# Attention scores as 64x64 blocks, and the neighbourhood attention's scores moved behind its projection

## The chip, the cores and the metric

The kernel runs on one NeuronCore of a Trainium2 chip. The metric is the device time of one execution in microseconds (us), from launch to end. TensorE (PE) multiplies matrices: it loads a stationary operand and streams a moving one past it, and its products land in PSUM, which has eight banks of 512 float32 columns on 128 partitions. VectorE (DVE), ScalarE (ACT) and GpSimd (POOL) work beside it, each through its own instructions in order. Engines wait for each other by semaphores.

## The reference

Two transformer models run one after the other on a sequence of 512 tokens with 1024 features. The first has two layers of feed-forward, hybrid mixer, feed-forward. Part of the mixer is sliding-window attention:

```python
scores = jnp.einsum('bnqkgd,bnskd->bnkgqs', qb, kb).astype(jnp.float32) * (HEAD_DIM ** -0.5)
```

The second model has two layers. Layer 0 is latent attention (16 heads; a query and a key have 64 plain features and 32 rotary ones, and the rotary key is shared by all heads). Layer 1 is neighbourhood attention (16 heads of 64; each query sees 256 context keys and a window of 256 grid keys). Both have 256 context tokens beside the 512 latent ones:

```python
s = jnp.concatenate([jnp.einsum('bqhd,bkhd->bhqk', qc, k_ctx),
                     jnp.einsum('bqhd,bkhd->bhqk', ql, k_lat)], -1)
p = softmax_f32(s.astype(jnp.float32) * scale).astype(v_lat.dtype)
```

## The kernel before, in words

Weights come by DMA, are split by ACT and POOL into a rounded high part and a low rest, and each projection is three fast matmuls per 128 rows of the contraction (lines 2603, 2604, 2605, called "fills" where they stand between the steps of an attention). The attention's own matmuls are plain float32. Each of those leaves two records of matmul in the trace, one after the other in time for one tile, and where two or four tiles of the array hold different blocks, the records of the tiles start 7 ns or so apart and stream side by side.

The order of TensorE's work in each attention is written out by hand, in one function per attention. A unit is a block of 128 queries of a pair of heads `g = 0, 1`, whose queries and keys lie on rows 0 to 63 and 64 to 127.

Latent attention (`mla_pe`): 4 passes of 12 units, 48 in all: 32 with latent queries, 16 with context queries. For unit u the loop issues `scores(u + 1)`, the first half of the transposition `turn(u, 0)` (line 2106: 64x64 blocks of probabilities against a diagonal that divides by the sum), `weigh(u - 1)` (line 2124: values), one fill into bank 7, and `turn(u, 1)`. Scores of a latent unit are four pairs of matmuls: plain rows with latent keys (L2085) and context keys (L2087), rotary rows with both (L2089, L2091); a context unit has L2080 and L2082. The rotary rows are 32 per head and lie at `h * 32`; the rotary key `kr` stands four times, once per 32 rows. `scores(u)` waits for the exponentials of unit u - 1 (L1426 on ACT).

Neighbourhood attention (`na_pe`): 32 units. Before the loop it issues six fills, `scores(0)` and one fill more. For unit u the loop issues `scores(u + 1)` (L2219, L2222), then the fill number u + 7 into bank 7 (there is one for u = 0 to 25), for which it first waits until the fill before it has been copied out of bank 7, then for u = 27 to 31 parts of the next projection (two to nine matmuls), `turn(u)` (L2236) and `weigh(u - 1)` (L2256). On ACT, `na_act` does for each u, in this order: `exps(u + 1)` (L1513), `fill_out` of fill u + 7 (L1490 to L1500), `copy(u)` (L1521), sometimes the split of a weight panel (L1589). On DVE, `na_dve` does `most(u + 1)` (bias added L3321, maximum L3326), `copy(u)` (L3340), `shares(u + 1)` (L3331, L3332). The lines of PE that the change moves:

```python
for u in range(NA_ALL):
    if u + 1 < NA_ALL:
        scores(u + 1)
    if na_fill(u) is not None:
        pe.wait_ge(sem["fill_out"], b["fill_out"] + u + NA_FIRST + 1)
        fill(u + NA_FIRST + 1, 7)
    ...
    turn(u)
    if u:
        weigh(u - 1)
```

The mixer's attention (`mixer_pe`): 8 units in each of two layers, each with fills, `scores(u + 1)` (L1875, L1877), `turn(u)` (L1894) and `values(u - 1)` (L1909), in this order.

Of the kernel before, what the change touches and what calls it, by code (L numbers as in the profile page):

```python
# [20 lines left out]
ds = bass.ds  # L21

P = 128
# [229 lines left out]
def mla_step(a):  # L253
    wq, wkv = weight_panels(a["mla_w_qb_2"][0]), weight_panels(a["mla_w_kvb_2"][0])
    n = NH // PER
    pairs, units = PER // 2 * 6, PER * 6

    def dma(i, j):

        w, per, first, second = ((wq, DQ, NOPE, ROPE), (wkv, P, NOPE, HD))[j]  # L260
        out = []
        for h in range(PER):
            out.append((("cols", h * first, first), w[:, :, ds(i * (PER * per) + h * per, first)]))
            out.append((("cols", PER * first + h * second, second), w[:, :, ds(i * (PER * per) + h * per + first, second)]))
        return out

    return dict(kind="mla", iters=n, shapes=[(3, PER * DQ), (2, PER * P)], dma=dma,
                totals=dict(fill_made=11 * n, fill_out=11 * n, q_rot=n,
                            s_made=pairs * n, s_max=units * n, s_exp=units * n, s_shared=units * n,
                            turned0=units * n, turned1=units * n, copied0=units * n, copied1=units * n,  # L270
                            s_weighted=pairs * n, s_kept=PER * n, h_hi=KD - 1, h_ready=KD - 1))
# [199 lines left out]
def build(nc, a, out):  # L471
# [101 lines left out]
    mean_m = sb("mean_m", [P, P])  # L573
    eps = sb("eps", [P, 2])
    spare = place[0]
# [64 lines left out]
    kn = sb("kn", [P, 2, T], at=h_at + 11264)  # L640
    kr = sb("kr", [P, T], at=h_at + 17408)
    vals = (sb("vals_even", [P, 6, PER * HD], at=g_raw_at), sb("vals_odd", [P, 6, PER * HD], at=h_at + 26624))
# [679 lines left out]
    def mla_in_act(st, b, act, split_hi):  # L1322
# [39 lines left out]
        for k in (3, 4):  # L1362
            rounded(k)
        act.wait_ge(sem["low_out"], b["low_out"] + 4)

        nc.scalar.activation(kr[:, 0:C], low_pe[:, 0:C], ACT.Copy).then_inc(sem["act_chain"], 1)

# [460 lines left out]
    def mixer_pe(st, b, pe, triple, first_panel):  # L1828
# [31 lines left out]
        def scores(u):  # L1860
            i, nh = u // 2, u % 2
            if u == 0:

                pe.wait_ge(sem["in_evac"], b["in_evac"] + 3)
            else:
                pe.wait_ge(sem["at_s_read"], b["at_s_read"] + u)
            if u == 4:

                pe.wait_ge(sem["in_evac"], b["in_evac"] + 5)
            for m in range(2):  # L1870
                n = 2 * nh + m
                for g in range(2):
                    q = mq[rows_at(g), i, n * P:(n + 1) * P]
                    if n == 0:
                        ins = nc.tensor.matmul(ps_g[:, g, P:2 * P], q, mk[rows_at(g), 0:P], start=True, stop=True)  # L1875
                    else:
                        ins = nc.tensor.matmul(ps_g[:, g, m * 2 * P:(m + 1) * 2 * P], q, mk[rows_at(g), (n - 1) * P:(n + 1) * P], start=True, stop=True)  # L1877
            ins.then_inc(sem["at_s"], 1)
# [126 lines left out]
    def mla_pe(st, b, pe, triple):  # L2005
# [55 lines left out]
        def scores(u):  # L2061
# [12 lines left out]
            qq = slice(q * P, (q + 1) * P)  # L2074
            low_rows = lambda g: slice(g * NOPE, (g + 1) * NOPE)
            rope_rows = lambda g: slice((2 * hp + g) * ROPE, (2 * hp + g + 1) * ROPE)
            first, second = (lambda g: ps_all[:, 2 * g, C:2 * C]), (lambda g: ps_all[:, 2 * g + 1, :])
            if ctx:
                for g in range(2):
                    nc.tensor.matmul(first(g), qcn[low_rows(g), hp, qq], kn[low_rows(g), hp, 0:C], start=True, stop=False)  # L2080
                for g in range(2):
                    ins = nc.tensor.matmul(first(g), qcr[i % 2][rope_rows(g), qq], kr[rope_rows(g), 0:C], start=False, stop=True)  # L2082
            else:
                for g in range(2):
                    nc.tensor.matmul(second(g), qn[low_rows(g), hp, qq], kn[low_rows(g), hp, C:T], start=True, stop=False)  # L2085
                for g in range(2):
                    nc.tensor.matmul(first(g), qn[low_rows(g), hp, qq], kn[low_rows(g), hp, 0:C], start=True, stop=False)  # L2087
                for g in range(2):
                    nc.tensor.matmul(second(g), qt[i % 2][rope_rows(g), qq], kr[rope_rows(g), C:T], start=False, stop=True)  # L2089
                for g in range(2):  # L2090
                    ins = nc.tensor.matmul(first(g), qr[i % 2][rope_rows(g), qq], kr[rope_rows(g), 0:C], start=False, stop=True)  # L2091
            ins.then_inc(sem["s_made"], 1)
# [78 lines left out]
    def na_pe(st, b, pe, triple, sum_squares):  # L2171
# [30 lines left out]
        def scores(u):  # L2202
# [11 lines left out]
            if u >= 2:  # L2214

                pe.wait_ge(sem["s_exp"], b["s_exp"] + u - 1)
            half = lambda g: slice(g * HD, (g + 1) * HD)
            for g in range(2):
                nc.tensor.matmul(ps_all[:, 2 * (u % 2) + g, 0:C], nq[half(g), pair, j * P:(j + 1) * P], nk[half(g), pair, 0:C], start=True, stop=True)  # L2219
            for g in range(2):  # L2220
                kk = nk[half(g), pair, C:T].rearrange("p (r n) -> p r n", n=GRID)[:, :, BAND[j]:BAND[j] + KC_]
                ins = nc.tensor.matmul(ps_all[:, 2 * (u % 2) + g, C:2 * C].rearrange("p (r n) -> p r n", n=KC_), nq[half(g), pair, j * P:(j + 1) * P], kk, start=True, stop=True)  # L2222
            ins.then_inc(sem["s_made"], 1)
# [46 lines left out]
        for u in range(NA_ALL):  # L2270
            if u + 1 < NA_ALL:
                scores(u + 1)
            if na_fill(u) is not None:
# [3 lines left out]
            for c, k in NA_PROJ.get(u, ()):  # L2277
# [950 lines left out]

    def rope(dve, ch, o, x_, swapped):

        V = nc.vector
        ch.step(V.tensor_tensor(o, x_, turns[:, 0, :], ALU.mult))
        ch.link(V.tensor_tensor(turned[:, :], swapped, turns[:, 1, :], ALU.mult))
        return V.tensor_tensor(o, o, turned[:, :], ALU.add)

    def mla_in_dve(st, b, dve, ch):
        V = nc.vector
        for n, (k0, k1, g) in enumerate(((0, 3, col["q_norm"]), (3, 5, col["kv_norm"]))):
# [7 lines left out]
        dve.wait_ge(sem["rope_in"], 48)  # L3246
        dve.wait_ge(sem["pe_rot"], b["pe_rot"] + 1)
        rope(dve, ch, kr[:, C:T], low_pe[:, C:T], ps_s[:, :]).then_inc(sem["pe_key"], 1)

# [6 lines left out]
    def mla_dve(st, b, dve, ch):  # L3256
# [38 lines left out]
        for g in range(2):  # L3295
            shares(0, g)
        U = PASSES * MLA_N
        for u in range(U):
# [58 lines left out]
    def _(dve):  # L3357
# [115 lines left out]

        n_gemv = [0, 0]
        for st in PLAN:
            b = st["base"]
# [241 lines left out]
```

## Time and profile before

| what | value |
|---|---|
| median of 3 runs | 3669.26 us (3668.59 to 3672.66) |
| span of the profiled execution | 3665.2 us |
| its own time as a run | not listed; the median is 4.1 us above the span |
| PE busy | 3609.4 us, 98% of the span |
| DVE, ACT, POOL busy | 1825.1, 1426.8, 1621.2 us |
| granted PE clock | nine tenths or more in each of the 40 slices |

Busy time counts a stretch once, however many records overlap in it. A matmul's record is longer than the time after which the next can start, so what a step costs on PE is read from start to start. A row of the timeline merges instructions of one line: its first column is the start of the first. 64\*128 is a stationary block of 64 rows and 128 columns.

### The profile page before, as it was taken

To read this page: it belongs to the slowest core of one execution; us is meant where nothing else is said; L and a number is where in the kernel's file an instruction comes from. 1 tells how busy PE (TensorE), PEld (TensorE's weight loads), DVE (VectorE), ACT (ScalarE), POOL (GpSimd) and SP (SyncE) were. 2 spreads that over 40 slices of the span, in tenths; PEclk is the share of its full clock that TensorE was granted. 3 is DMA by queue.
4 is the path that set the end of the run, shared out by engine and by line. 5 is a ranking of instruction groups with operands and counts; after the bars stand their busy time and mean duration, and the time that the engine had idled before them with its cause. 6 is when DMAs were issued, how large, how long until landed. Compare 5 with 4: busy or idle time off the path is not lost.

```text
span 3665.2 us, 65989 instructions
## 1 busy us (share of the span) xinstructions
PE 3609.4 (98%) x25844; PEld 3005.3 (82%) x25844; DVE 1825.1 (50%) x3439; ACT 1426.8 (39%) x2027; POOL 1621.2 (44%) x1330
## 2 busy tenths in 40 slices
PE   7999999999999999999999999999999999999998
PEld 6888878888888887888897767888889988888887
DVE  6435565554775655763645444444427433343333
ACT  4322364322432245432234444443436533435333
POOL 2444444445454444445541003345458843334543
PEclk9999999999999999999999999999999999999999
DMA  8665525575555442445420001122245522212332
GB/s 258 190 186 162 149 59 161 184 223 168 183 176 189 151 115 65 157 155 159 139 74 20 15 25 36 58 94 90 90 136 165 159 69 70 75 58 92 92 99 85
DMA packets 560423, 442.81 MB, mean 121 GB/s; under 512 B 60452, under 2 KB 558157, under 8 KB 559949
## 3 DMA queue, kind: packets, MB, share of 16 engines
q1 hardware_dynamic: 560205, 439.73, 39.0%
q8 instruction: 158, 2.59, 0.3%
q14 instruction: 60, 0.49, 0.0%
HBM read 432.65 MB, written 2.83 MB: 119 GB/s over the span
## 4 chain that ended last, share of the span: by engine, by line
PE 92%; DVE 3%; ACT 2%; issue 1%; POOL 1%; SPq 1%; DMA 0%; DVEq 0%; ACTq 0%; POOLq 0%
PE ps_all L2603 26%; PE ps_all L2604 25%; PE ps_all L2605 25%; PE ps_all L2106 2%; PE ps_all L2124 1%; PE ps_all L2588 1%; PE ps_all L2085 1%; PE ps_all L2575 1%; PE ps_all L2089 1%; PE ps_all L2236 1%; PE ps_all L2576 1%; PE ps_all L2256 1%; POOL w_lo L1012 1%; DVE prod_t L3549 0%; PE ps_all L2219 0%
## 5 line engine op out<-in xcount | busy, mean ns | idle before, releaser
L1012 POOL TENSOR_TENSOR w_lo<-raw,w_hi 128x512 fp32r<-128x512 f32 (+2 forms) x1124 | 1341.5, 1225 | 1882.2 <-ACT w_hi L1589 1802.2
L2603 PE MATMUL ps_all<-h_hi,w_hi 128*128 128x512 f32 (+1 forms) x2600 | 1010.4, 389 | 2.8 <-POOL w_lo L1012 2.2
L2605 PE MATMUL ps_all<-h_hi,w_lo 128*128 128x512 f32 (+1 forms) x2600 | 1004.1, 386 | 0.0
L2604 PE MATMUL ps_all<-h_lo,w_hi 128*128 128x512 f32 (+1 forms) x2600 | 1003.9, 386 | 0.0
L1589 ACT ACTIVATE w_hi<-raw 128x2048 fp32r<-128x2048 f32 (+4 forms) x277 | 471.4, 1702 | 1275.5 <-PE ps_all L2605 1268.4
L2603 PEld LDWEIGHTS ps_all<-h_hi,w_hi 128*128 128x128 f32 x2600 | 488.7, 188 | 111.0 <-issue 11.1
L2605 PEld LDWEIGHTS ps_all<-h_hi,w_lo 128*128 128x128 f32 x2600 | 488.6, 188 | 98.7
L2604 PEld LDWEIGHTS ps_all<-h_lo,w_hi 128*128 128x128 f32 x2600 | 488.9, 188 | 96.9
L2603 PE MATMUL ps_all<-hid_hi,w_hi 128*128 128x512 f32 (+1 forms) x1282 | 473.2, 369 | 2.1 <-POOL w_lo L1001 1.7
L2605 PE MATMUL ps_all<-hid_hi,w_lo 128*128 128x512 f32 (+1 forms) x1282 | 469.5, 366 | 0.0
L2604 PE MATMUL ps_all<-hid_lo,w_hi 128*128 128x512 f32 (+1 forms) x1282 | 469.4, 366 | 0.0
L3375 DVE SCALAR_TENSOR_TENSOR ps_all<-g_raw,c_col,ps_all 128x256 f32<-128x256 f32 x832 | 335.7, 482 | 0.0
L2603 PEld LDWEIGHTS ps_all<-hid_hi,w_hi 128*128 128x128 f32 x1282 | 241.7, 188 | 43.0 <-POOL w_lo L1001 2.2
L2604 PEld LDWEIGHTS ps_all<-hid_lo,w_hi 128*128 128x128 f32 x1282 | 241.7, 189 | 39.8 <-issue 0.5
L2605 PEld LDWEIGHTS ps_all<-hid_hi,w_lo 128*128 128x128 f32 x1282 | 241.7, 189 | 39.2
L3577 DVE SCALAR_TENSOR_TENSOR x<-ps_all,modc,x 128x512 f32<-128x512 f32 (+1 forms) x91 | 68.0, 747 | 413.3 <-PE ps_all L2605 407.4
L3549 DVE TENSOR_TENSOR prod_t<-gate_t,ps_all 128x1024 f32<-128x1024 f32 x44 | 53.7, 1220 | 265.5 <-PE ps_all L2605 265.5
L3552 DVE TENSOR_TENSOR hid_lo<-prod_t,hid_hi 128x1024 f32 (+3 forms) x71 | 100.6, 1417 | 107.1 <-ACT hid_hi L1705 107.1
L2603 PE MATMUL ps_all<-c_hi,w_hi 128*128 128x256 f32 x400 | 114.7, 287 | 2.5 <-DVE prod_t L3549 2.5
L3193 DVE SCALAR_TENSOR_TENSOR prod_t<-ps_all,colv,prod_t 128x511 f32<-128x511 f32 (+1 forms) x54 | 33.1, 655 | 163.1 <-ACT prod_t L1756 163.1
L2604 PE MATMUL ps_all<-c_lo,w_hi 128*128 128x256 f32 x400 | 113.8, 284 | 0.0
L2605 PE MATMUL ps_all<-c_hi,w_lo 128*128 128x256 f32 x400 | 113.5, 284 | 0.0
(460 smaller groups left out, 5129.0 us busy)
## 6 DMA issues: line engine op xcount, KB each, us to landing
raw<-in_w_ffn_gu_dram SPq DMA_DIRECT2D x88, 1024.0 KB, 5.2
g_raw<-in_w_mod_dram SPq DMA_DIRECT2D x66, 1024.0 KB, 7.4
raw<-in_ffn_w_in_dram SPq DMA_DIRECT2D x54, 1024.0 KB, 5.0
g_raw<-in_ada_w_dram SPq DMA_DIRECT2D x48, 1024.0 KB, 5.3
raw<-in_w_ffn_down_dram SPq DMA_DIRECT2D x32, 768.0 KB, 4.7
raw<-in_w_ffn_down_dram SPq DMA_DIRECT2D x32, 640.0 KB, 4.3
raw<-in_ffn_w_out_dram SPq DMA_DIRECT2D x22, 768.0 KB, 4.7
raw<-in_ffn_w_out_dram SPq DMA_DIRECT2D x20, 640.0 KB, 4.3
```

The costliest lines, as they stand in the source:

```text
L1012: ins = nc.gpsimd.tensor_tensor(v(w_lo), raw_view(st, i, j)[:, first:end, :], v(w_hi).bitcast(F32), ALU.subtract)
L1589: nc.scalar.activation(w_view(w_hi, j % 2, st["shapes"][j]), raw_view(st, i, j), ACT.Copy).then_inc(sem["w_split_hi"], 1)
L2085: nc.tensor.matmul(second(g), qn[low_rows(g), hp, qq], kn[low_rows(g), hp, C:T], start=True, stop=False)
L2089: nc.tensor.matmul(second(g), qt[i % 2][rope_rows(g), qq], kr[rope_rows(g), C:T], start=False, stop=True)
L2106: ins = nc.tensor.matmul(ps_all[keys_, 4 + qh, t * HD:(t + 1) * HD], prob[n % 2][rows_, g, w], diag[rows_, n % 2, g, rows_], start=True, s ...
L2603: nc.tensor.matmul(o, whi, mhi, start=first, stop=False)
L2604: nc.tensor.matmul(o, whi, mlo, start=False, stop=False)
L2605: return nc.tensor.matmul(o, wlo, mhi, start=False, stop=last)
L3375: ins = nc.vector.scalar_tensor_tensor(o, w, s, sofar, ALU.mult, ALU.add)
L3549: nc.vector.tensor_tensor(prod_t[:, :, 0:N], gate_t[:, :, 0:N], other, ALU.mult).then_inc(sem["product"], 1)
L3552: nc.vector.tensor_tensor(hid_lo[:, w].rearrange("p (c n) -> p c n", c=2), prod_t[:, :, 0:N], hid_hi[:, w].rearrange("p (c n) -> p c n", c ...
L3577: nc.vector.scalar_tensor_tensor(v, ps_d[:, j, 0:N], modc[:, ds(st["gate"] + j + i * 2, 1)], v, ALU.mult, ALU.add).then_inc(sem[f"down{j}" ...
```

## The change

Scores in all three attentions are made in quarters: the 128 queries are cut in two halves, each half goes to its own 64 columns of the array and 64 partitions of PSUM, and the block is 64x64. So that the rotary rows fill 64 too, the rotary query columns are placed so that heads 0 and 2 lie on rows 0 to 63 and heads 1 and 3 on rows 64 to 127, and the rotary key is kept in two copies, each with the rows of the head that is not meant set to zero by a mask of ones and zeros (two new columns of `eps`, eight memsets at the start). DVE makes the first copy before the units (`rope_keys`) and the second after the shares of unit 0 (`rope_keys_odd`); ACT's copy of the context part goes. In the neighbourhood attention `scores(u + 1)` is issued after the fill and the projection parts, right ahead of `turn(u)`; nothing changes there on ACT or DVE.

```diff
+            place = h if j else h // 2 + 2 * (h % 2)
+            out.append((("cols", PER * first + place * second, second), w[:, :, ds(i * (PER * per) + h * per + first, second)]))
...
-        act.wait_ge(sem["low_out"], b["low_out"] + 4)
-        nc.scalar.activation(kr[:, 0:C], low_pe[:, 0:C], ACT.Copy).then_inc(sem["act_chain"], 1)
...
+                    for qh in range(2):
+                        q = mq[rows_at(g), i, n * P + qh * HD:n * P + (qh + 1) * HD]
+                        if n == 0:
+                            ins = nc.tensor.matmul(ps_g[rows_at(qh), g, P:2 * P], q, mk[rows_at(g), 0:P], start=True, stop=True)
+                        else:
+                            ins = nc.tensor.matmul(ps_g[rows_at(qh), g, m * 2 * P:(m + 1) * 2 * P], q, mk[rows_at(g), (n - 1) * P:(n + 1) * P], start=True, stop=True)
...
+            if u == MLA_N // 2:
+                pe.wait_ge(sem["pe_key"], b["pe_key"] + 1)
...
+            first, second = (lambda g, h: ps_all[low_rows(h), 2 * g, C:2 * C]), (lambda g, h: ps_all[low_rows(h), 2 * g + 1, :])
+            def quarters(o, q_, k_, start):
+                for g in range(2):
+                    for h in range(2):
+                        ins = nc.tensor.matmul(o(g, h), q_[low_rows(g), q * P + h * NOPE:q * P + (h + 1) * NOPE], k_[low_rows(g), :], start=start, stop=not start)
+                return ins
...
+                quarters(first, qcn[:, hp, :], kn[:, hp, 0:C], True)
+                ins = quarters(first, qcr[i % 2], kr_ctx[hp], False)
...
+                quarters(second, qn[:, hp, :], kn[:, hp, C:T], True)
+                quarters(first, qn[:, hp, :], kn[:, hp, 0:C], True)
+                quarters(second, qt[i % 2], kr_lat[hp], False)
+                ins = quarters(first, qr[i % 2], kr_ctx[hp], False)
...
+                for qh in range(2):
+                    nc.tensor.matmul(ps_all[half(qh), 2 * (u % 2) + g, 0:C], nq[half(g), pair, queries(qh)], nk[half(g), pair, 0:C], start=True, stop=True)
...
         for u in range(NA_ALL):
-            if u + 1 < NA_ALL:
-                scores(u + 1)
...
                 proj_part(st["following"], pe, triple, c, k)
+            if u + 1 < NA_ALL:
+                scores(u + 1)
             turn(u)
...
+    def rope_keys(dve, ch, b):
         V = nc.vector
-        ch.step(V.tensor_tensor(o, x_, turns[:, 0, :], ALU.mult))
-        ch.link(V.tensor_tensor(turned[:, :], swapped, turns[:, 1, :], ALU.mult))
-        return V.tensor_tensor(o, o, turned[:, :], ALU.add)
+        mask = [eps[:, 2 + m:3 + m] for m in range(2)]
+        dve.wait_ge(sem["rope_in"], 48)
+        dve.wait_ge(sem["low_out"], b["low_out"] + 4)
+        ch.step(V.scalar_tensor_tensor(kr_lat[0][:, :], low_pe[:, C:T], mask[0], turns[:, 0, :], ALU.mult, ALU.mult))
+        V.tensor_scalar(kr_ctx[0][:, :], low_pe[:, 0:C], mask[0], None, ALU.mult)
+        dve.wait_ge(sem["pe_rot"], b["pe_rot"] + 1)
+        ch.link(V.tensor_tensor(turned[:, :], ps_s[:, :], turns[:, 1, :], ALU.mult))
+        V.scalar_tensor_tensor(kr_lat[0][:, :], turned[:, :], mask[0], kr_lat[0][:, :], ALU.mult, ALU.add).then_inc(sem["pe_key"], 1)
+    def rope_keys_odd(dve, ch):
+        V = nc.vector
+        mask = eps[:, 3:4]
+        ch.link(V.scalar_tensor_tensor(kr_lat[1][:, :], low_pe[:, C:T], mask, turns[:, 0, :], ALU.mult, ALU.mult))
+        V.tensor_scalar(kr_ctx[1][:, :], low_pe[:, 0:C], mask, None, ALU.mult)
+        V.scalar_tensor_tensor(kr_lat[1][:, :], turned[:, :], mask, kr_lat[1][:, :], ALU.mult, ALU.add).then_inc(sem["pe_key"], 1)
...
+        rope_keys_odd(dve, ch)
...
+        for m in range(2):
+            for q in range(PER):
+                ch.step(nc.vector.memset(eps[q * Q32:(q + 1) * Q32, 2 + m:3 + m], 1.0 - abs(q % 2 - m)))
```

## Rows read from the trace of the kernel before

**Rows 1.** The page: chain that ended last, by engine

```profile
PE 92%; DVE 3%; ACT 2%; issue 1%; POOL 1%; SPq 1%; DMA 0%; DVEq 0%; ACTq 0%; POOLq 0%
```

**Rows 2.** Latent scores: records, ns min/median/max; idle of PE before L2085, times

```profile
L2085 PE MATMUL ps_all<-kn,qn x128: 589/626/694, 1937.5 to 2240.7; 64*128 64x512 f32 x128
...
  ACT prob_even L1426: 3.7, 5
  ACT prob_odd L1426: 1.8, 6
```

**Rows 3.** Timeline of PE, one latent unit: start, us, work, records

```profile
2000.39 0.93 PE L2106 MATMUL ps_all<-diag,prob_odd 64*64 64x64 f32 x48
2001.25 1.13 PE L2085 MATMUL ps_all<-kn,qn 64*128 64x512 f32 x4
2002.21 0.60 PE L2087 MATMUL ps_all<-kn,qn 64*128 64x256 f32 x4
2002.74 1.13 PE L2089 MATMUL ps_all<-kr,qt_even 32*128 32x512 f32 x4
2003.70 0.60 PE L2091 MATMUL ps_all<-kr,qr_even 32*128 32x256 f32 x4
2004.23 0.93 PE L2106 MATMUL ps_all<-diag,prob_even 64*64 64x64 f32 x48
```

**Rows 4.** Timeline of PE, a context unit's transposition

```profile
1975.78 0.46 PE L2106 MATMUL ps_all<-diag,prob_even 64*64 64x64 f32 x16
```

**Rows 5.** Float32 matmuls of the whole array, back to back (line 2404)

```profile
L2404 PE MATMUL ps_all<-squares,mean_m x16: 378/379/379, 2495.2 to 2498.4; 128*128 128x256 f32 x16
...
L2404 PE MATMUL ps_all<-squares_h,mean_m x16: 590/593/593, 2729.2 to 2735.7; 128*128 128x512 f32 x16
```

**Rows 6.** Timeline of PE, scores and transposition in the mixer

```profile
1376.73 1.13 PE L1877 MATMUL ps_all<-mk,mq 64*128 64x256 f32 x8
```

**Rows 7.** Timeline of DVE at the start of the latent units

```profile
1948.05 0.96 DVE L3277 TENSOR_REDUCE stat<-ps_all 128x1 f32<-128x768 f32 x1 [4.10 <-PE ps_all L2091]
```

**Rows 8.** Timeline of PE, one round of the neighbourhood attention

```profile
3038.93 0.70 PE L2219 MATMUL ps_all<-nk,nq 64*128 64x256 f32 x4
...
3040.00 0.50 PE L2603 MATMUL ps_all<-h_hi,w_hi 128*128 128x512 f32 x1
...
3045.68 1.16 PE L2236 MATMUL ps_all<-diag_n,prob_n 64*64 64x64 f32 x64
3046.77 0.66 PE L2256 MATMUL ps_all<-prob_nt,nv_even 128*64 128x128 f32 x8
...
3047.80 0.70 PE L2219 MATMUL ps_all<-nk,nq 64*128 64x256 f32 x4
```

**Rows 9.** Timeline of DVE, then of ACT, in the same round

```profile
3040.11 0.70 DVE L3321 TENSOR_TENSOR ps_all<-ps_all,bias_m 128x512 f32<-128x512 f32 x1 [0.40 <-PE ps_all L2222]
...
3042.18 0.69 ACT L1513 ACTIVATE prob_n<-ps_all,stat 128x512 f32<-128x512 f32 x1 [3.55 <-DVE stat L3326]
...
3043.43 0.20 ACT L1513 ACTIVATION_READ_ACCUMULATOR prob_n<-ps_all,stat 128x1 f32 x1
3045.79 0.60 ACT L1498 ACTIVATE nk<-ps_all 128x512 f32<-128x512 f32 x1 [2.17 <-PE ps_all L2605]
```

**Rows 10.** Waits of PE in the neighbourhood attention's stretch (2930 to 3250)

```profile
PE ps_all L2236 <- DVE diag_n L3332: 0.2, 1, 0.2
```

**Rows 11.** Timeline, a late round without a whole fill

```profile
3206.44 0.20 ACT L1513 ACTIVATION_READ_ACCUMULATOR prob_n<-ps_all,stat 128x1 f32 x1
3206.54 0.60 ACT L1521 ACTIVATE prob_nt<-ps_all 128x512 f32<-128x512 f32 x1
...
3207.22 0.69 DVE L3321 TENSOR_TENSOR ps_all<-ps_all,bias_m 128x512 f32<-128x512 f32 x1
...
3211.30 0.69 DVE L3321 TENSOR_TENSOR ps_all<-ps_all,bias_m 128x512 f32<-128x512 f32 x1
3211.43 0.46 PE L2236 MATMUL ps_all<-diag_n,prob_n 64*64 64x64 f32 x16
```

**Rows 12.** Timeline of PE, two idle gaps between projections

```profile
550.83 0.51 PE L2603 MATMUL ps_all<-yl_hi,w_hi 128*128 128x512 f32 x1 [1.94 <-POOL w_lo L1012]
...
1457.92 0.74 PE L2603 MATMUL ps_all<-yl_hi,w_hi 128*128 128x512 f32 x1 [1.96 <-POOL w_lo L1012]
```

**Rows 13.** Windows behind those gaps: busy us of PE, PEld, DVE, ACT, POOL; PEclk; DMA

```profile
1458.00:1461.40 3.40, 3.40 (x8) 2.67 (x9) 0.00 (x0) 1.01 (x2) 3.36 (x3) 0.50 0.64 210
...
550.10:553.50 3.40, 2.67 (x12) 2.23 (x13) 0.24 (x1) 1.84 (x3) 3.21 (x4) 1.00 0.42 125
```

More of the change, by code:

```diff
@@ L263, in dma @@
             out.append((("cols", h * first, first), w[:, :, ds(i * (PER * per) + h * per, first)]))
-            out.append((("cols", PER * first + h * second, second), w[:, :, ds(i * (PER * per) + h * per + first, second)]))
+            place = h if j else h // 2 + 2 * (h % 2)
+            out.append((("cols", PER * first + place * second, second), w[:, :, ds(i * (PER * per) + h * per + first, second)]))
         return out
     return dict(kind="mla", iters=n, shapes=[(3, PER * DQ), (2, PER * P)], dma=dma,
-                totals=dict(fill_made=11 * n, fill_out=11 * n, q_rot=n,
+                totals=dict(fill_made=11 * n, fill_out=11 * n, q_rot=n, pe_key=1,
                             s_made=pairs * n, s_max=units * n, s_exp=units * n, s_shared=units * n,
@@ L573, in build @@
     mean_m = sb("mean_m", [P, P])
-    eps = sb("eps", [P, 2])
+    eps = sb("eps", [P, 4])
     spare = place[0]
@@ L640, in build @@
     kn = sb("kn", [P, 2, T], at=h_at + 11264)
-    kr = sb("kr", [P, T], at=h_at + 17408)
+    kr_lat = (sb("kr_lat_even", [P, S], at=h_at + 17408), sb("kr_lat_odd", [P, S], at=hid + 47104))
+    kr_ctx = (sb("kr_ctx_even", [P, C], at=h_at + 19456), sb("kr_ctx_odd", [P, C], at=tmp + 15360))
     vals = (sb("vals_even", [P, 6, PER * HD], at=g_raw_at), sb("vals_odd", [P, 6, PER * HD], at=h_at + 26624))
@@ L1872, in scores @@
                 for g in range(2):
[L1873 to L1877, printed above, removed]
+                    for qh in range(2):
[4 more added lines that the diff above has]
+                            ins = nc.tensor.matmul(ps_g[rows_at(qh), g, m * 2 * P:(m + 1) * 2 * P], q, mk[rows_at(g), (n - 1) * P:(n + 1) * P], start=True, stop=True)
             ins.then_inc(sem["at_s"], 1)
@@ L2078, in scores @@
+            def quarters(o, q_, k_, start):
[3 more added lines that the diff above has]
+                return ins
             if ctx:
[L2079 to L2082, printed above, removed]
-            else:
[L2084 to L2091, printed above, removed]
@@ L2217, in scores @@
             half = lambda g: slice(g * HD, (g + 1) * HD)
+            queries = lambda qh: slice(j * P + qh * HD, j * P + (qh + 1) * HD)
             for g in range(2):
-                nc.tensor.matmul(ps_all[:, 2 * (u % 2) + g, 0:C], nq[half(g), pair, j * P:(j + 1) * P], nk[half(g), pair, 0:C], start=True, stop=True)
+                for qh in range(2):
+                    nc.tensor.matmul(ps_all[half(qh), 2 * (u % 2) + g, 0:C], nq[half(g), pair, queries(qh)], nk[half(g), pair, 0:C], start=True, stop=True)
             for g in range(2):
                 kk = nk[half(g), pair, C:T].rearrange("p (r n) -> p r n", n=GRID)[:, :, BAND[j]:BAND[j] + KC_]
-                ins = nc.tensor.matmul(ps_all[:, 2 * (u % 2) + g, C:2 * C].rearrange("p (r n) -> p r n", n=KC_), nq[half(g), pair, j * P:(j + 1) * P], kk, start=True, stop=True)
+                for qh in range(2):
+                    ins = nc.tensor.matmul(ps_all[half(qh), 2 * (u % 2) + g, C:2 * C].rearrange("p (r n) -> p r n", n=KC_), nq[half(g), pair, queries(qh)], kk, start=True, stop=True)
             ins.then_inc(sem["s_made"], 1)
@@ L3245, in mla_in_dve @@
                 ins.then_inc(sem["low_full"], 1)
-        dve.wait_ge(sem["rope_in"], 48)
-        dve.wait_ge(sem["pe_rot"], b["pe_rot"] + 1)
-        rope(dve, ch, kr[:, C:T], low_pe[:, C:T], ps_s[:, :]).then_inc(sem["pe_key"], 1)
+        rope_keys(dve, ch, b)
     def share(dve, ch, s_, ready, o):
```

4 lines of the change are left out of this document (removed).

## The prediction

> **What bounds the kernel now.** I read the chain of waits first: TensorE holds 92% of it [rows 1], so its time sets the end, and a change is worth what it adds to or takes from TensorE's sequence, start to start. Then I read the two attentions' stretches for TensorE's own waits. In the latent attention it waits for the exponentials 11 times, 5.5 us in all [rows 2]; in the neighbourhood attention its one wait inside the loop is 0.2 us [rows 10]. Both are bound by TensorE, with little room to spare in the first. Last I read single rounds on the timelines, for what lies between two kinds of matmul, and for the time at which ACT and DVE do what TensorE will ask for next.
>
> **Latent scores as quarters.** A float32 record of the whole array costs 0.43 us for 512 columns (6.5 us over 15 steps) and 0.215 for 256 [rows 5]. The two heads already stream side by side: four records of 512 columns take 0.96 us, not 1.7 [rows 3]. Four quarters side by side stream the same columns in the same time, so the blocks themselves gain nothing; what goes is the price of changing the block shape. A latent unit's scores take 2004.23 - 2001.25 = 2.98 us [rows 3] and stream 4 x 0.43 + 4 x 0.215 = 2.58: 0.40 over. The transposition's 48 records take 0.86 us to the next start [rows 3]; 16 take 0.46 where 48 take 0.93 [rows 4], so 32 cost 0.47, 48 cost 0.70, and 0.16 is the price of coming and going. With one shape from `turn(u, 1)` through both scores to the next `turn` all of it goes once a unit: 0.56 us, for 48 units 26.9. (L2085 has 128 records, four a unit: 32 latent units [rows 2]; the other 16 are context units, with the same three changes of shape.)
>
> At the 11 places where TensorE already waits for exponentials, what is saved ahead of the scores only lengthens the wait: the 0.16 and the 0.10 by which the last step (2003.70 to 2004.23, 0.53) exceeds its 0.43 [rows 3]. 11 x 0.26 = 2.9 comes off: **-24.0 us**. Bounds: if quarters of 512 columns streamed only two at a time, 2.58 would become 5.16 and everything would be slower by far (a rival below); no row shows four blocks with a moving operand this long. The nearest row is the transposition, where groups of four records cost 0.47/8 = 0.059 us for a double pass over 64 columns, which is the full rate (0.43/8 = 0.054). I take full rate.
>
> The Trainium skill's page "TensorEngine Tiling (Array Packing)", Key Properties, says that changing the tiling mode drains the engine. By a drain alone, about 0.10 us a change as in that last step, the sum would be 3 x 0.10 x 48 = 14.4 us; the trace shows nearly twice that, because the second load behind a change isn't hidden either, and I go by the rows.
>
> **Mixer.** The same for `scores` and `turn` alone: 1377.80 - 1376.73 = 1.07 us [rows 6] against 4 x 0.215 = 0.86 gives 0.21. Two layers of 8 units: **-3.2 us** (0 to -4).
>
> **Keys on DVE.** The first copy adds one short operation ahead of `pe_rot` and drops ACT's; the queries' rotation and the evacuation of the keys stand behind it, so nothing or a few tenths. The second copy's three operations lie behind the shares of unit 0, where DVE idles 4.10 us before the next maximum [rows 7]; three such operations, at 0.7 us each like a bias addition of 512 columns [rows 9], are 2.1. TensorE asks for them only at unit 6. Without that cover they would cost 2.1 once. Memsets and the order of query columns: before and beside the first loads, nothing. Sum 0 (-0.5 to +2).
>
> **Neighbourhood scores moved behind the fill.** This is the term that decides. As quarters they save one change of shape a round, 0.2 us. But look at ACT's order: `exps(u + 1)`, then the copying out of fill u + 7. In the round shown the scores come first (3038.93), the exponentials are over at 3043.63 while the fill still runs (3040.00 to 3045.68), and the fill is copied out at 3045.79, at once [rows 8, 9]. `turn`, `weigh` and the next scores hide the copy, and the next fill finds bank 7 free. After the change the scores come behind the fill. The fill is complete, but ACT stands in `exps` and waits for these scores' maximum; the next fill waits for ACT. From scores to next fill the chain is now: to the bias addition 1.18 [rows 8, 9], less 0.05 for the entry in one shape; to the first exponential 2.07; both exponentials to the next ACT operation 1.35 (the read at 3043.43 plus 0.10, as in the late round [rows 9, 11], less 3042.18); the copy 0.60 [rows 9]; hand-over about 0.05, my estimate. Together 5.20 us. TensorE's own work there is scores 0.91, `turn` 1.04, `weigh` 1.03 [rows 8]: 2.98. It waits 2.2 us.
>
> A round was 3047.80 - 3038.93 = 8.87 us [rows 8]. It becomes 5.68 (the fill, start to start) + 5.20 = 10.88: +2.01. There are 26 fills in the loop, and each but the first waits: 25 x 2.01 = 50.3. Round 0 has no `weigh` to lie beside the chain (+1.0), and the first fill loses the scores ahead of it (-0.3). Behind the last fill nothing long covers unit 26: from its scores to its `turn` the chain needs 1.13 + (3211.43 - 3207.22) = 5.34 us [rows 11] where TensorE has 0.91 + 1.04 + 1.03 + 0.91 = 3.9; with the round behind it I take +1.9. The last rounds go in DVE's and ACT's own circle, 3211.30 - 3207.22 = 4.08 us [rows 11], and gain nothing. Sum **+52.9 us** (45 to 58: the chain may be shorter or longer by 0.2 a round).
>
> **The clock.** A 1.96 us gap of TensorE was followed by a stretch at a granted clock of 0.50, that is 1.2 GHz instead of 2.4; a gap of 1.94 was not [rows 12, 13]. The gaps to come are of this size, 2.2 us. The low stretch was 3.4 us, and would fall on a fill, so it costs 3.4 x 0.5 = 1.7 us each. From 0 (none of 25) to 42.5 (all). One in two of the gaps shown led to it; since each one lengthens its round and shifts the next against whatever the clock goes by, I take 10: **+17 us**.
>
> On this the Trainium skill speaks the other way: "TensorE: Matmul & The Clock Gate", in its closing table of goals, asks only that idle gaps stay below a length which these gaps do not reach. By it this term would be 0; the row of the 1.96 us gap disagrees.
>
> **Sum.** -24.0 - 3.2 + 0 + 52.9 + 17.0 = +42.7 us. On the profiled execution's span that is 3665.2 + 42.7 = 3707.9; the median of the runs is 4.1 above that span, so I forecast 3712 us.
>
> **Rivals.**
> (A) The same wait, but the clock stays up: 3669.3 + 25.7 = 3695. For it: the 1.94 us gap. Against: the 1.96 us one. 27%.
> (B) The same, and the clock falls after nearly every gap: 3669.3 + 25.7 + 42.5 = 3737. Against it: each stretch of low clock moves the next gap. 9%.
> (C) The other side: the wait doesn't come, because ACT's copy is ready in time. It decides at a chain of 2.98 us from scores to next fill; below that only savings are left: 24 + 3.2 + 31 rounds x 0.2 = 33 us faster, 3636. For it: TensorE waits for almost nothing there now, and the exponentials end 2 us ahead of the fill. Against it: that lead is measured from scores which start before a 5.68 us fill; ACT works in order, and its maximum alone takes 3.2 us from the start of the scores (1.13 + 2.07). 6%.
> (D) Quarters with long moving operands stream two at a time. Then 32 x 2.58 + 16 x 0.86 + 32 x 0.86 + 16 x 0.86 = 138 us more: about 3850. Against it: the transposition's rate. 4%.
>
> **How the numbers follow.** My forecast has 50%, the rivals 46%; the remaining 4% are mixtures, half of them near no change. Anything beyond 0.2% (7 us) a measurement of this kernel can tell from no change. Faster: C, 0.06. Same: 0.02. Slower: all else, 0.92. The range reaches down to A with its NA term at the lower end (3695 - 8, and 3 for the latent term: 3684) and up to B with 5 to spare (3742). It leaves out C and D and the fringes of A and B, together under 2 in 10.
>
> **What would show it.** In the profile after: fills of line 2603 in the neighbourhood attention sit idle before their first record, released by ACT's copies, about 25 times and 2.2 us each; rounds of 10.9 us, or 12.6 with a low clock; granted clock below 1 between about 2930 and 3290. Latent scores with starts 2.58 us apart from the next transposition, and no extra step at the rotary rows. The prediction is wrong if those fills start without idle time (C), if a quarter's group of four takes 0.86 us (D), or if the latent attention shrinks by less than 20 us because DVE or ACT takes the bound there.

## The result and the profile after

The changed kernel takes 3722.1 us, the median of 4 runs (3720.6 to 3723.4), where the kernel before takes 3668.9 on the same chip (3667.5 to 3672.7): a ratio of 1.0147, 95% interval 1.0133 to 1.0162. It is slower by 53 us; the forecast was 3712, the range 3684 to 3742. The profiled execution's span is 3721.0 us against 3665.2.

I divide the span's difference of 55.8 us by stretches of TensorE, each from the start of the first scores to the start of the last record of a transposition:

| stretch | before | after | difference | forecast |
|---|---|---|---|---|
| latent attention | 323.6 | 304.6 | -19.0 | -24.0 |
| mixer, two layers | 77.4 + 77.3 | 2 x 76.8 | -1.2 | -3.2 |
| neighbourhood attention | 260.8 | 333.4 | +72.6 | +69.9 (52.9 order, 17 clock) |
| all the rest | | | +3.4 | 0 |

The page of the kernel after, the chain that ended last: TensorE held 92% of it before [rows 1].

```profile
PE 88%; DVE 5%; ACT 3%; issue 2%; POOL 1%; SPq 1%; DMA 0%; DVEq 0%; ACTq 0%; POOLq 0%
```

The chain now runs over DVE and ACT at more places. The waits of TensorE in the neighbourhood attention say where (2944 to 3278; line waited for, releaser: us in total, times, longest). I show the entries that ACT's copies of a fill end; the others come to 4.0 us in 5 waits, nearly all in the last rounds. Before, the list held one entry inside the loop, of 0.2 us [rows 10]:

```profile
PE ps_all L2608 <- ACT nk L1497: 16.1, 7, 3.1
PE ps_all L2608 <- ACT nq L1494: 13.7, 7, 2.2
PE ps_all L2608 <- ACT nv_odd L1489: 8.6, 4, 2.2
PE ps_all L2608 <- ACT nk L1499: 6.7, 3, 2.2
PE ps_all L2608 <- ACT nv_odd L1501: 4.4, 2, 2.2
PE ps_all L2608 <- ACT nv_even L1489: 4.3, 2, 2.2
PE ps_all L2608 <- ACT nv_even L1501: 2.2, 1, 2.2
```

Those are 56.0 us in 26 waits. Every one is the first matmul of a fill that waits for ACT's copying out of the fill before it. One round on TensorE's timeline (start, us, work, records, idle time before):

```profile
3018.02 0.66 PE L2223 MATMUL ps_all<-nk,nq 64*64 64x256 f32 x8
3018.50 0.61 PE L2227 MATMUL ps_all<-nk,nq 64*64 64x256 f32 x8
3018.93 1.11 PE L2241 MATMUL ps_all<-diag_n,prob_n 64*64 64x64 f32 x64
3019.98 0.66 PE L2261 MATMUL ps_all<-prob_nt,nv_even 128*64 128x128 f32 x8
3020.46 0.61 PE L2261 MATMUL ps_all<-prob_nt,nvb_even 128*64 128x128 f32 x8
3023.23 0.50 PE L2608 MATMUL ps_all<-h_hi,w_hi 128*128 128x512 f32 x1 [2.16 <-ACT nq L1494]
```

And ACT's in the same round, from the first exponential to the copy that TensorE waits for:

```profile
3021.24 0.69 ACT L1512 ACTIVATE prob_n<-ps_all,stat 128x512 f32<-128x512 f32 x1 [6.18 <-DVE stat L3343]
3021.83 0.19 ACT L1512 ACTIVATION_READ_ACCUMULATOR prob_n<-ps_all,stat 128x1 f32 x1
3021.92 0.68 ACT L1512 ACTIVATE prob_n<-ps_all,stat 128x512 f32<-128x512 f32 x1
3022.49 0.20 ACT L1512 ACTIVATION_READ_ACCUMULATOR prob_n<-ps_all,stat 128x1 f32 x1
3022.58 0.60 ACT L1494 ACTIVATE nq<-ps_all 128x512 f32<-128x512 f32 x1
```

The copy of `nq` takes 0.60 us, and its data were complete at about 3018.1, when the fill ended. It starts 4.5 us later because ACT stood ahead of it, idle for 6.18 us, waiting for the maximum of scores that had only just been made. Before, the same kind of copy started 0.1 us after the fill's end [rows 8, 9].

### The profile page after: what moved, and what is told of

It reads as the page before. It is cut to its first block, busy times and chain, and to the rows that moved or that the text cites. A ratio compares the mean times of both kernels' runs of the same rounds, so it can differ in the third digit from the quotient of the medians.

```text
span 3721.0 us, 68048 instructions
## 1 busy us (share of the span) xinstructions
PE 3602.6 (97%) x26868; PEld 3010.8 (81%) x26868; DVE 1820.4 (49%) x3451; ACT 1418.1 (38%) x2026; POOL 1620.1 (44%) x1330
## 4 chain that ended last, share of the span: by engine, by line
PE 88%; DVE 5%; ACT 3%; issue 2%; POOL 1%; SPq 1%; DMA 0%; DVEq 0%; ACTq 0%; POOLq 0%
PE ps_all L2608 26%; PE ps_all L2609 25%; PE ps_all L2610 25%; PE ps_all L2083 3%; PE ps_all L2108 1%; PE ps_all L2126 1%; PE ps_all L2593 1%; DVE stat L3343 1%; PE ps_all L2580 1%; PE ps_all L2581 1%; ACT prob_n L1512 1%; POOL w_lo L1014 1%; DVE ps_all L3338 1%; DVE prod_t L3569 0%; PE ps_all L2223 0%
## 5 line engine op out<-in xcount | busy, mean ns | idle before, releaser
L1512 ACT ACTIVATE prob_n<-ps_all,stat 128x512 f32<-128x512 f32 x64 | 43.4, 683 | 226.4 <-DVE stat L3343 226.3
L3338 DVE TENSOR_TENSOR ps_all<-ps_all,bias_m 128x512 f32<-128x512 f32 x32 | 22.4, 698 | 208.0 <-PE ps_all L2227 208.0
```

The source lines that it names most:

```text
L1512: ins = nc.scalar.activation(prob_n[:, u % 2, g, :], ps_all[:, 2 * (u % 2) + g, :], ACT.Exp, bias=at(1), accum_out=at(2))
L3338: V.tensor_tensor(pair[:, :, C:2 * C], pair[:, :, C:2 * C], bias_m[:, n % BIAS_AHEAD, :, :], ALU.add).then_inc(sem["s_biased"], 1)
```

## The experiments

**1. The two halves of the change apart.** The first kernel is the changed one with the scores back ahead of the fill; the second is the kernel before with only the move.

```
e1 (the kernel after)                     e2 (the kernel before)
  for u in range(NA_ALL):                   for u in range(NA_ALL):
+     if u + 1 < NA_ALL:                  -     if u + 1 < NA_ALL:
+         scores(u + 1)                   -         scores(u + 1)
      ... fill, projections ...                 ... fill, projections ...
-     if u + 1 < NA_ALL:                  +     if u + 1 < NA_ALL:
-         scores(u + 1)                   +         scores(u + 1)
      turn(u)                                   turn(u)
```

> The changed kernel with one part undone: the neighbourhood attention's scores(u + 1) stand again ahead of the fill; all quarters and the two masked keys stay. Theory (the loss is the order, the quarters gain): latent units about 18 us shorter than before, mixer 1 to 2, neighbourhood 32 x 0.05 = 1.6 for the shorter entry into 64x64 blocks; 3669 - 21 = 3648 us (3643 to 3655), no fill of the neighbourhood attention idle for ACT's copies. Rival (the quarters themselves cost there, or the masked keys do): at or above 3669, with neighbourhood rounds longer than 8.87 us.

> The kernel before with one part of the change: scores(u + 1) of the neighbourhood attention behind the fill, everything else as before (64x128 blocks). Theory: as many changes of block shape a round as before, so the whole wait and nothing saved there: 25 rounds x 2.06 + 4 = 55 us, and 8 to 14 stretches of low clock at 1.7 us: 3669 + 75 = 3744 us (3725 to 3760). Rival (the order does no harm by itself): 3669 within 0.2%.

Measured: quarters in the old order 3649.5 us, 0.9949 (0.9936 to 0.9963) of before; the order alone 3744.6, 1.0210 (1.0194 to 1.0225). Apart they come to -19.3 and +75.8, together +56.5, against +53.2 for both at once, which is within the intervals. The neighbourhood attention takes 259.6 us in the first and 333.8 in the second, which has 11 stretches of 3.4 us at the lower clock, as the kernel after has. So the quarters help, the move hurts, and neither needs the other. The move alone shows the same waits, a little shorter, since the old block shape keeps TensorE busy 0.1 to 0.2 us longer in a round. The first of these lines is the order alone's; before it stands the last record of `weigh`:

```profile
3026.24 0.61 PE L2256 MATMUL ps_all<-prob_nt,nvb_even 128*64 128x128 f32 x8
3028.88 0.50 PE L2603 MATMUL ps_all<-h_hi,w_hi 128*128 128x512 f32 x1 [2.04 <-ACT nk L1500]
```

**2. The wait taken away on ACT's side, the move kept.** If the cause is ACT's order, and not the place of the scores as such, then swapping two calls on ACT removes the wait.

```
  for u in range(NA_ALL):            # na_act
+     fill_out(u + NA_FIRST + 1, 7)
      if u + 1 < NA_ALL:
          exps(u + 1)
-     fill_out(u + NA_FIRST + 1, 7)
      copy(u)
```

> The changed kernel with two lines of ACT exchanged in the neighbourhood attention: fill_out of fill u + 7 ahead of exps(u + 1). Theory (the fill waits only because ACT stands in exps ahead of the copy): the idle time before the fills goes, rounds of 8.87 - 0.2 = 8.67 us, no low clock there: about 3722 - 72 - 6 = 3644 us (3638 to 3652), faster than before and than the kernel with the old order. Rival (the wait comes from the late scores by another way, the maximum on DVE or the bank): at least 20 us of idle time before fills stay, 3690 or more.

Measured: 3648.3 us, 0.9946 (0.9932 to 0.9959); the neighbourhood attention 259.2 us, 74.2 less than in the kernel after. TensorE's timeline, then ACT's:

```profile
3008.55 0.66 PE L2223 MATMUL ps_all<-nk,nq 64*64 64x256 f32 x8
3009.04 0.61 PE L2227 MATMUL ps_all<-nk,nq 64*64 64x256 f32 x8
3009.47 1.11 PE L2241 MATMUL ps_all<-diag_n,prob_n 64*64 64x64 f32 x64
3010.51 0.66 PE L2261 MATMUL ps_all<-prob_nt,nv_even 128*64 128x128 f32 x8
3011.00 0.61 PE L2261 MATMUL ps_all<-prob_nt,nvb_even 128*64 128x128 f32 x8
3011.53 0.50 PE L2608 MATMUL ps_all<-h_hi,w_hi 128*128 128x512 f32 x1
```

```profile
3008.66 0.60 ACT L1497 ACTIVATE nk<-ps_all 128x512 f32<-128x512 f32 x1 [3.61 <-PE ps_all L2610]
3011.78 0.69 ACT L1512 ACTIVATE prob_n<-ps_all,stat 128x512 f32<-128x512 f32 x1 [2.52 <-DVE stat L3343]
```

The order of TensorE's work is that of the kernel after; the copy now starts at 3008.66, right behind the fill's last record (3008.24 to 3008.63), and the next fill starts without idle time. ACT's place in line was the whole of the 25 waits in the rounds; the 0.7 us of the first fill stay. The kernel's total is 4 us above what I had put down, and the list of TensorE's waits of this kernel in 3150 to 3250 says where a part of it lies:

```profile
PE ps_all L2241 <- DVE diag_n L3349: 1.9, 3, 1.3
PE ps_all L2608 <- POOL h_lo L1021: 1.4, 1, 1.4
```

These lie in the last rounds, where no whole fill covers the way from scores to `turn`. In the rounds that have a fill the kernel gains 0.2 us each against the kernel before, as put down (8.66 for 8.87, and 8.93 for 9.12).

**3. The late rounds given their old order.** From the kernel above, in rounds without a fill (from 26 on) the scores go ahead again; in a second kernel, from round 25 on, and ACT's calls with them.

```
e5: if na_fill(u) is None and u + 1 < NA_ALL: scores(u + 1)   # ahead of the fill
    ...
    if na_fill(u) is not None: scores(u + 1)                  # ahead of turn(u)
e9: the same with u >= 25 and u < 25; ACT: exps(u + 1) first where u >= 25
```

> The kernel with the copy first, and in the rounds without a whole fill (u = 26 to 31) the scores again ahead of the parts of the next projection. The fast order for the fill rounds saved 0.2 us each of 25 there, yet the whole stretch was no shorter than with the old order (259.2 us against 259.6), so some 4 us must go in the last rounds. Theory (there DVE's and ACT's circle is the bound, and late scores lengthen it): 255.5 us for the stretch, 3648.3 - 4 = 3644.5 us. Rival (the last rounds are no longer for another reason, ACT's high parts or POOL's): 3648, the stretch 259.

> The kernel with the copy first, with scores ahead of the fill and the copy behind the exponentials from u = 25 on instead of u = 26. Theory (behind the last fill, the transposition of unit 26 waits 1.3 us for DVE's diagonal because nothing long lies between its scores and itself; with the scores ahead of that 3 us fill the wait goes): neighbourhood stretch 257.9 - 1.2 = 256.7 us, the whole 3644 us, the fastest of all. Rival (the wait moves to the next transpositions, since DVE and ACT have their own circle of 4.08 us there): 257.9, 3645.4.

Measured: 3645.4 us (0.9937, 0.9923 to 0.9950) and 3646.4 us (0.9942, 0.9928 to 0.9955). The neighbourhood attention takes 257.9 and 256.9 us. The transposition of round 26 still waits for its diagonal matrix in the first, half as long in the second. TensorE's timelines of the two, a line from each:

```profile
3180.03 1.16 PE L2241 MATMUL ps_all<-diag_n,prob_n 64*64 64x64 f32 x64 [1.31 <-DVE diag_n L3351]
```

```profile
3182.55 1.16 PE L2244 MATMUL ps_all<-diag_n,prob_n 64*64 64x64 f32 x64 [0.64 <-DVE diag_n L3354]
```

The late rounds hold a part of the loss: 1.3 us come back, where I had put down 3.7, then another 1.0, where I had put down 1.2. In e9 the wait is halved and not gone. The totals of the two can't be told apart. With e9, e5 is the fastest kernel of the study, 23 us below the kernel before and 77 below the one after; from e1 it differs by 4 us, of which 1.7 are its shorter neighbourhood attention and 1.8 a latent attention without one low clock (below).

**4. The gap filled with other work.** The clock's share is told from the wait's by keeping the wait and giving TensorE something to do in it. Ahead of the fill two matmuls (in a second kernel one) of 512 columns write to a bank that nobody reads at that time.

```
  if na_fill(u) is not None:
+     if u:
+         pe.wait_ge(sem["s_exp"], b["s_exp"] + u)
+         for r in range(2):         # e7: one matmul
+             nc.tensor.matmul(ps_all[:, 2 * ((u + 1) % 2), :], mean_m, h_hi[:, 0:S], ...)
      pe.wait_ge(sem["fill_out"], b["fill_out"] + u + NA_FIRST + 1)
```

> The changed kernel with two float32 matmuls of 512 columns (0.43 us a record, four records, 1.7 us) put on TensorE ahead of each wait for ACT's copy, into a bank of scores that is free; they compute nothing that is used. Theory (low clock follows the idle gap): gaps of about 0.5 us are left, the wait ends when it did, rounds of 10.9 us; the low stretches within the neighbourhood attention go, at most 2 left, 3722 - 20 = 3702 us (3697 to 3708). Rival (the clock falls because the small blocks of the attention load the array little, whatever the gap): the low stretches stay, 3722.

> The changed kernel with one float32 matmul of 512 columns (0.86 us) ahead of each wait for ACT's copy, where the kernel with filled gaps had two; it computes nothing that is used. Gaps of about 1.35 us are left. Theory (low clock follows gaps of the size of 1.9 us and more): no low stretch in the neighbourhood attention or hardly one, 3706 us as with two. Rival (each gap has its chance, in proportion to its length): 6 to 8 low stretches, 3715 to 3718.

Measured: 3706.3 us with two (1.0104, 1.0088 to 1.0119), 3707.1 with one (1.0105, 1.0089 to 1.0120); the neighbourhood attention 316.5 and 318.1 us. TensorE's timeline with two, the end of a gap:

```profile
3017.26 1.98 PE L2280 MATMUL ps_all<-h_hi,mean_m 128*128 128x512 f32 x4
3019.49 0.50 PE L2611 MATMUL ps_all<-h_hi,w_hi 128*128 128x512 f32 x1 [0.25 <-ACT nq L1494]
```

From scores (3014.28) to fill the way is 5.21 us, as in the kernel after (3018.02 to 3023.23): the added matmuls change nothing of the wait's end. Only the granted clock differs. The windows over the whole stretch (us, then busy us of PE, PEld, DVE, ACT and POOL, granted clock, DMA share, GB/s), of the kernel after, of the one with two matmuls, of the one with one:

```profile
2944.00:3278.00 334.00, 274.09 (x4006) 231.57 (x4007) 101.03 (x160) 103.23 (x219) 106.64 (x112) 0.94 0.21 57
```

```profile
2945.00:3262.00 317.00, 304.85 (x4107) 233.47 (x4107) 101.13 (x161) 103.43 (x220) 106.53 (x112) 1.00 0.22 60
```

```profile
2943.00:3262.00 319.00, 285.37 (x4059) 225.86 (x4059) 101.05 (x160) 103.34 (x219) 106.99 (x112) 0.99 0.22 59
```

In the kernel after, 11 stretches of 3.4 us at the lower of the two levels, 1.2 GHz, follow upon 25 gaps, 24 of about 2.2 us and the first of 3.1. With both matmuls the gaps are mostly 0.25 us and no stretch follows. With one they are mostly 1.1 us and one stretch is left, at 2962.7, behind the longest gap, that of the first round:

```profile
2962.45 0.39 PE L2610 MATMUL ps_all<-ch_hi,w_hi 128*128 128x256 f32 x1 [2.06 <-ACT nk L1497]
```

The first gap is one of the eleven, so 10 of the 24 gaps of 2.2 us led to a low stretch; in e2, with gaps of 2.0 us and a first one of 2.9, it is 11 of 25 again. The waits end at the same place in all three kernels here, so it is TensorE's idleness in them that brings the clock down, and the 16.9 us between the kernel after and the one with two matmuls are the clock's (333.4 - 316.5): 1.54 us for each of the 11. The length of the gap alone doesn't decide: the gap of 1.94 us that had no low stretch behind it before [rows 12, 13] is 1.94 to 1.96 us long in all eleven kernels, and has one in e2, e4, e5 and e8. One such stretch of the kernel after, behind its gap and the window ahead of it:

```profile
2997.20:3000.60 3.40, 1.24 (x14) 1.00 (x11) 1.60 (x4) 2.42 (x6) 0.57 (x1) 1.00 0.01 2
3000.70:3004.10 3.40, 3.40 (x19) 3.40 (x18) 0.00 (x0) 0.00 (x0) 0.00 (x0) 0.51 0.02 5
```

The first window is the gap, 1.24 us busy of 3.40; in the second TensorE is busy throughout at a granted clock of 0.51, in 19 records.

**5. The rotary rows as before.** From e1, the widened rows go back to 32x128 blocks (with the single keys' buffer, ACT's copy and the old order of the query columns), so that each latent unit again has two changes of block shape around them. The edit for a latent unit's rows:

```
- quarters(second, qt[i % 2], kr_lat[hp], False)
- ins = quarters(first, qr[i % 2], kr_ctx[hp], False)
+ for g in range(2):
+     nc.tensor.matmul(ps_all[:, 2 * g + 1, :], qt[i % 2][rope_rows(g), qq], kr[rope_rows(g), C:T], ...)
+ for g in range(2):
+     ins = nc.tensor.matmul(ps_all[:, 2 * g, C:2 * C], qr[i % 2][rope_rows(g), qq], kr[rope_rows(g), 0:C], ...)
```

> The kernel with quarters and the old order, with the rotary rows of the latent attention as before: 32 rows, one key kr, blocks of 32x128 without masks. Theory (each change of block shape costs about 0.1 us of drain and 0.05 to 0.1 us behind it): of the 0.56 us a unit only the change from transposition to scores is saved, 0.2 us, and the two around the rotary rows stay; latent attention about 314 us instead of 304.7, 3649.5 + 10 = 3659 us. Rival (the gain is all in the first change, or in streaming four blocks): 3650.

Measured: 3660.5 us, 0.9974 (0.9964 to 0.9984), 11.0 above e1; the latent attention 316.1 us against 304.7 in e1 and 323.6 before. Of the 19 us, 7.6 belong to the one change, from the transposition into the scores, that quarters of the latent rows alone take away, and 11.4 to the two changes around the rotary rows. With the clock at one level the rotary rows' share would be 13: e1, as the kernel after, has a low stretch inside the latent attention, and this kernel has none. The scores of a unit on TensorE's timeline here:

```profile
2001.33 1.47 PE L2083 MATMUL ps_all<-kn,qn 64*64 64x512 f32 x16
2002.73 1.13 PE L2094 MATMUL ps_all<-kr,qt_even 32*128 32x512 f32 x4
2003.70 0.60 PE L2096 MATMUL ps_all<-kr,qr_even 32*128 32x256 f32 x4
```

The latent rows take 1.40 us to the next start for 1.29 of streaming, the change's 0.11; the step behind it takes 0.97 for 0.86 (0.96 in [rows 3]). The widened rows, half of them zeros, stream in no more time than these.

**6. The mixer alone.** From e5, the mixer's scores as before.

```
- for qh in range(2):
-     ... ps_g[rows_at(qh), g, ...], q half qh ...
+ ... ps_g[:, g, ...], all of q ...
```

> The kernel with the copy first and the old order in the last rounds, with the mixer's scores as before (64x128). One look, for the length of the mixer's attention from its first scores to its last transposition. Theory (quarters save 0.2 us a unit, but in two units a layer the transposition waits for DVE's diagonals and gives it back): 77.3 us a layer instead of 76.8, as in the kernel before; the whole time 1 us longer, less than runs differ. Rival (the quarters gain nothing in the mixer): 76.8.

Measured, in one run: 3648.7 us, and a layer takes 77.3 us against 76.8 in e5. The stretch tells what the total can't: 0.6 us a layer.

## Why the prediction was right, by its steps

On the spans the change cost 13 us more than forecast (55.8 for 42.7), and the parts of that have the same sign: 2.7 in the order's term, 5.0 in the latent one, 2.0 in the mixer's, 3.4 outside the three attentions, where I had nothing. Only the clock's term met its size, and that partly by chance. The mechanism is the one forecast.

**The order's term, +52.9: right, and for the reason given.** Measured +55.6 with the clock held up (e4's 316.47 less 260.84). The chain from scores to next fill was put at 5.20 us and takes 5.21; the gap at 2.2 and is 2.16; a round at 10.9 and takes 10.87 to 10.95, and 12.5 to 12.7 where the clock is low (12.6 forecast). About half of the rounds take 11.15 to 11.21 us: they were 9.12 before and not 8.87, which I had taken for all; the difference, 2.0, is the same. That the chain could be foretold so closely has a simple ground: every piece of it stood in the trace before, only in another order, and no operation was new. That the sum comes within 0.01 is luck, since two of the pieces, of 0.05 us each, were my estimates. The 25 waits came out as said, that of round 0 with 3.1 us among them, where no `weigh` lies beside the chain; the first fill, which I had wait for nothing, waits 0.7 us, the 26th of the list. The 2.7 us too little lie at the two ends and in the rounds: 0.9 up to the first transposition, 1.1 in the rounds behind the last fill (3.0 for 1.9), 0.8 in all the rounds between. e3 shows that the waits are ACT's order alone: with the copy first, 74 us go, the low clock's 17 among them.

**The clock's term, +17: right in size (16.9), on a chance of one in two.** I took 10 low stretches of 1.7 us; there are 11 of 1.54 (why not 1.7 isn't settled). e4 and e7 show that the idle time was their cause. That 11 came where I took 10 is luck in part: I had one gap with and one without to go by. The rule of the Trainium skill's page "TensorE: Matmul & The Clock Gate", in the table of goals of its section "Why this matters for your kernels", allows idle gaps up to about 3 us. By it only the first gap, of 3.1 us, could have led to a low stretch; the 10 behind gaps of 2.2 us disagree with it. Rival A (3695) was the case without low stretches, and e4, at 3706.3, is what it comes to on the chip. On the spans e4 is 13 us above rival A's sum, of which the order's term has 2.7, the latent one 3.4, the mixer's 2.0 and the rest of the kernel 5.

**The latent term, -24.0: right in kind, too large by 5.** The unit's scores take 2.58 us, as put down, by TensorE's timeline of the kernel after:

```profile
1998.23 1.47 PE L2083 MATMUL ps_all<-kn,qn 64*64 64x512 f32 x16
1999.52 1.04 PE L2083 MATMUL ps_all<-kr_lat_odd,qt_even 64*64 64x512 f32 x8
2000.38 0.61 PE L2083 MATMUL ps_all<-kr_ctx_odd,qr_even 64*64 64x256 f32 x8
2000.81 0.88 PE L2108 MATMUL ps_all<-diag,prob_even 64*64 64x64 f32 x48
```

Quarters stream at the full rate (rival D is out). From start to start of their scores 15 units save the whole 0.56 us and 8 save 0.50. Two things I had not in the sum, and a third came out otherwise. The first: a context unit's scores now stream for only 0.86 us, and in all 16 of these units the transposition behind them waits for DVE's copy of the one before; the unit saves 0.40. Those scores and the transposition on TensorE, and DVE's copy:

```profile
1966.97 0.61 PE L2083 MATMUL ps_all<-kn,qcn 64*64 64x256 f32 x8
1967.40 0.61 PE L2083 MATMUL ps_all<-kr_ctx_even,qcr_even 64*64 64x256 f32 x8
1967.95 0.93 PE L2108 MATMUL ps_all<-diag,prob_odd 64*64 64x64 f32 x48
```

```profile
1967.24 0.56 DVE L3302 COPY prob_t_even<-ps_all 128x384 f32<-128x384 f32 x1 [1.95 <-PE ps_all L2108]
```

The copy ends at 1967.80; the transposition starts at 1967.95 where streaming would have it at 1967.83. It starts 0.15 us behind the copy in each of the 16 units; before, the first of them had 0.54. The second: near the end one stretch at half clock costs 1.6 us. It stands in the kernel after, in e1 and in e3, and not in e4, e5, e7, e8 and e9, whose latent attention takes 303 us. The third: some units end in a wait of the next scores for exponentials and save 0.23 to 0.31, so each loses 0.25 to 0.33 where I took off 0.26 [rows 2]; there are 8 of them, not 11. Two units near the end, one a context unit, come out longer by 0.1 and by 1.3 (the low stretch), and the last unit, a context one too, saves 0.29. Together: 15 x 0.56 + 8 x 0.50 + 14 x 0.40 + 9 x 0.28 - 1.4 = 19.1, against 19.0 measured. The copy is what the term had wrong, 2.6 us of it: I asked of each saving whether TensorE waited there already, and not whether it would begin to. I had named a latent attention that shrinks by less than 20 us, because DVE or ACT takes the bound, as a sign of being wrong. It shrank by 19.0; without the low stretch it is 20.6, so that sign came half true, through DVE's copy.

**Why more than a drain went.** A drain is what the Trainium skill's page "TensorEngine Tiling (Array Packing)" names in Key Properties. By a drain of 0.10 us a change alone, 14.4 us would have been saved. The measured 19.0, and 20.6 without the low stretch, lie above that; the unit's 0.56 us for three changes is what the rows gave. The weight loads show the other part. The first line is the entry into the latent scores in the kernel before, the second that of the kernel after:

```profile
2001.25 0.30 PEld L2085 LDWEIGHTS ps_all<-kn,qn 64*128 64x128 f32 x4
1998.17 0.21 PEld L2083 LDWEIGHTS ps_all<-kn,qn 64*64 64x64 f32 x8
```

Before, the first pair of loads comes together with the first pair of matmuls (2001.25, [rows 3]), and the second pair 0.11 us behind it (four loads of 0.18 us fill 0.30). After, the first loads come 0.06 us ahead of the first matmul (1998.23), under the transposition's last records.

**The mixer, -3.2: a third of it came.** The scores are 0.2 us shorter, but in two units of a layer the transposition then waits for DVE's diagonal matrices. TensorE's timeline of the kernel after, one of these:

```profile
477.01 0.45 PE L1875 MATMUL ps_all<-mk,mq 64*64 64x128 f32 x8
477.28 0.61 PE L1877 MATMUL ps_all<-mk,mq 64*64 64x256 f32 x8
478.26 1.15 PE L1894 MATMUL ps_all<-diags,att 64*64 64x64 f32 x62 [0.37 <-DVE diags L3128]
```

Four waits, the longest of 0.4 us, give 1.3 of 3.2 back, by the list of waits; 1.2 came. The remaining 0.7 us is not accounted for.

**The keys on DVE, 0: right, to about 0.1 us, and what is left over is the clock's.** No wait on them stands in the list of TensorE's waits, and DVE's three added operations aren't named by any wait. From the mixer's last transposition to the first latent scores it takes 495.4 us before and 497.1 after; but it takes 497.0 in e6, which has the old keys with ACT's copy. So the 1.7 us are not the keys'. Ahead of the latent attention the projection runs at a lower granted clock than before. The windows, of the kernel before and then of the one after:

```profile
1895.00:1925.00 30.00, 30.00 (x191) 28.05 (x190) 3.63 (x8) 9.79 (x16) 11.19 (x10) 0.90 0.18 38
```

```profile
1895.00:1925.00 30.00, 30.00 (x178) 28.06 (x178) 3.62 (x8) 9.66 (x16) 11.15 (x10) 0.84 0.18 38
```

That is 0.06 x 30 = 1.8 us. Between the latent and the neighbourhood attention it is the same again: 699.8 us before, 701.3 after, with 10.2 us at the lower clock for 6.8. The two make 3.3 of the 3.4 us left over, and the sum had no term for low stretches outside the neighbourhood attention. Every kernel with the latent scores as quarters has 6.8 us at the lower clock near 1905, the two without (before and e2) have 3.4. Why is open, since this stretch lies ahead of the first of those scores.

**Rival C**, the wait that doesn't come, fell by the chain that I had put against it: ACT works in order. The chain was not below 2.98 us but 5.21. e3, which takes the exponentials out of it, comes to 3648 where C had 3636; the smaller latent and mixer gains (7 us), the late rounds and the 3 us outside the attentions are between them.

## What to carry to other kernels

When a producer is moved behind a consumer on one engine, read the in-order queue of every other engine that serves both: here a 0.6 us copy stood behind exponentials whose input had just been moved 5.7 us later, and made TensorE wait 2.2 us a round. The pieces of such a new chain stand in the old trace and can be added up; here the cure was the same swap on the other engine's side. Price an idle gap of TensorE by what the clock does after it as well, and of every saving ask who is late next: the shorter scores uncovered a copy and a diagonal matrix on DVE, in a third of the latent units and a quarter of the mixer's.

## What the runs showed of the hardware

- Four 64x64 blocks with a moving operand of 512 float32 columns stream side by side at the full rate: a unit's four steps, two of 512 and two of 256 columns with two records each, take 2.58 us, which is 4 x 0.43 + 4 x 0.215 (the kernel after).
- A float32 matmul of 512 columns whose 64 rows are half zero takes the 0.86 us of streaming that one of 32 rows takes. The two changes of block shape around the 32-row matmuls cost 11.4 us over the latent attention (e6 against e1). Behind a change the first loads are not hidden, and the second ones come 0.11 us later (the kernel before).
- Of 24 gaps of about 2.2 us, 10 led to a stretch of 3.4 us at 1.2 GHz, and so did the one of 3.1 us; gaps of 1.1 or 0.25 us in the same places did not, with TensorE busy on results that nobody reads, though one of 2.06 us did (e7). One and the same gap of 1.95 us led to such a stretch in 4 of 11 kernels. Two matmuls without a purpose bought back 16 us.
